# A second attention whose keys are formed beside its values, in one fused kernel of two decoder stages

## The chip, the cores and the metric

One core of a Trainium2 chip runs the whole program. The metric is device time in microseconds, from launch to end, the median of several executions; lower is better. TensorE multiplies, VectorE and ScalarE work on tiles and on TensorE's results, GpSimd (POOL) and SyncE issue transfers. Each engine takes its own instructions in the order written; only semaphores tie one engine to another.

## The reference, cut to what matters

The program computes an even layer (convolution and block attention), an odd layer (the attention of this case), a gated delta rule layer, cross attention and a feed-forward layer, over 256 tokens of width 2048 in float32. The part around the change is the odd layer:

```python
z = _rmsnorm(x, norm_g) @ w_in
cq, ckv, ik, iw, gate = _split_cols(z, [512, 256, 64, 16, 2048])
q = (cq @ w_qb).reshape(b, t, 16, 128)
q_lat = jnp.einsum('bthd,hdc->bthc', q, w_uk)          # 256 latent columns a head
...                                                    # index scores choose 64 keys for each query
s = jnp.einsum('bqhc,bqkc->bqhk', ql_c, kv) * scale
p = jax.nn.softmax(s, axis=-1)
o_lat = jnp.einsum('bqhk,bqkc->bqhc', p, kv)
o = jnp.einsum('bthc,hcd->bthd', o_lat, w_uv).reshape(b, t, DSA_WIDTH)
return (o * jax.nn.silu(gate)) @ w_out
```

There are 16 heads of 128. The scores of a head are q w_uk ckv^T. They can be had by taking q into the latent space (256 wide) and multiplying by ckv, or by taking ckv out to keys of 128 (k = ckv w_uk^T) and multiplying q by those. The choice of keys enters as a bias of -1e30 on what is not chosen; the kernel finds it with 16 rounds of top-8 (8 for each half of the queries).

## The kernel before, in words

**Projections.** Every large weight is split in two float32r halves, a high part (ScalarE's `split`, L1355) and a remainder (VectorE's `split`, L2090), and each product takes three matmuls. A *unit* (L717) is 128 output columns; its result is drained by ScalarE (`drain`, L1371) and summed by VectorE (`post`, L2124). There are two accumulator banks, so a unit waits until the sum of the unit two before it is made (`emptied`, L439). Projections that are added to x are *wide units* (`wide_unit`, L776) of 24 matmuls of 512 columns. Units are handed on through four weight slots: ScalarE splits unit n when unit n-4 has been multiplied.

**The odd layer's order.** `o_small` (cq, ckv, ik, iw), `o_gate0`, `o_iq`, `o_gate1` with the index scores beside it (`index_beside`), then `o_q` (16 units of q, 128 columns each, so one head a unit), the attention loop, and `o_out` (16 wide units). VectorE's `top_k` rounds (L2531) stand between its splits and sums of `o_q`.

**Values beside q.** TensorE forms the values of a later head (`values`, L986: ckv times w_uv, four plain float32 matmuls of 128 columns, each of which the profile shows as two records) behind every second unit of `o_q`, seven heads ahead (`V_AHEAD`), and in the loop's steps those of head s+7. ScalarE copies them out (`values`, L1751).

**The loop** (TensorE L1008, ScalarE L1776, VectorE L2565), one step per head, each engine in its own written order. TensorE's step s: latent queries of head s (L1019, two matmuls of 256 columns); scores of head s-1 from the copied latent queries (L1030); turn of the probabilities of head s-3 (L1039, three transposes); values by probabilities of head s-4 (L1048 and L1049); values of head s+7 (L993). ScalarE's step: copy of the latent queries (L1781), exponential with its sum (L1632), copy of the turned probabilities (`pt_step`, L1641), copy of values (L1756), and in some steps the high part of a unit of `o_out` or of four gated heads (`gate_round`, L1766). VectorE's step: scaling and bias of the scores (`mask_step`, L2401), row maxima (L2405), division by the sum (`scale_step`, L2412 and L2414), product with the gate (L2573), and in some steps the remainder of a unit of `o_out` (L2098) or of four gated heads (`gate_rest`, L2559). Scores of a head wait until the bias of the head two before has been added; probabilities have three places.

The first wide units of `o_out` stand in the last steps (16, 18 and 19): wide unit j needs the gated heads 4j to 4j+3, split.

**Transfers.** POOL loads w_uk and w_uv by head (`load_uk`, `load_uv`, L592 and L598), from when `o_gate1` has been multiplied, and later the gain of the norm behind this layer (L618). SyncE loads the weights of the projections into two ring places.

## Time and profile before

| what | before |
|---|---|
| median of 3 runs | 2435.91 us (2435.5 to 2436.31) |
| the profiled execution | 2435.91 us |
| its span | 2434.2 us |
| TensorE matmuls busy | 2397.7 us, 99% |
| TensorE weight loads busy | 2071.3 us, 85% |
| VectorE busy | 1611.9 us, 66% |
| ScalarE busy | 1166.3 us, 48% |
| POOL busy | 156.6 us, 6% |
| share of TensorE in the chain that ended last | 95% |

The page reads: one row for each engine with its busy time and share of the span; a strip of 40 equal slices with the busy tenths of each engine and the granted clock of TensorE (9 is 90% or more, and all 40 slices have it); the chain that ended last, followed back from the last instruction. Matmul records overlap, since matmuls are pipelined: a matmul's price in a row of matmuls is the distance from one start to the next, not its own duration. In the trace the units of `o_q` end at 653.5 us, the loop's steps run from 654.57 to 728 us, and the other wide units of `o_out` follow.

### The profile page before, as it was taken

The numbers are of one execution on the slowest core, as the hardware profiler recorded it, in microseconds if no ns is written. First come the engines' busy times: TensorE is split into PE (matmuls) and PEld (weight loads), VectorE is DVE, ScalarE is ACT, GpSimd is POOL, SyncE is SP. The second block draws the span as 40 slices with busy tenths as digits, with TensorE's granted clock in tenths as the row PEclk, the third lists the DMA queues.
The fourth block names the chain that finished last, engine by engine and source line by source line (L and its number), as shares of the span: only waits on it lengthen the run. The fifth ranks groups of instructions, "written<-read, shape, count | busy, mean of one in ns | idle before, by whom it ended". The sixth has DMA issues, their size and how long they took to land.

```text
span 2434.2 us, 35338 instructions
## 1 busy us (share of the span) xinstructions
PE 2397.7 (99%) x14059; PEld 2071.3 (85%) x14059; DVE 1611.9 (66%) x2030; ACT 1166.3 (48%) x1407; POOL 156.6 (6%) x142
## 2 busy tenths in 40 slices
PE   7999999999999999999999999999999999999998
PEld 6888988888888888888988888888888888888887
DVE  6999676555665787597665445455777467755764
ACT  6433674545455654643554344345554334433433
POOL 1000000000200100000000000000122002200220
PEclk9999999999999999999999999999999999999999
DMA  8555446454425556553075555444655565656554
GB/s 249 186 194 190 157 139 231 138 191 146 158 86 205 159 177 188 188 159 121 25 251 176 184 195 173 139 146 165 200 180 202 183 200 175 204 178 204 175 183 143
DMA packets 337333, 422.43 MB, mean 174 GB/s; under 512 B 8478, under 2 KB 263212, under 8 KB 336700
## 3 DMA queue, kind: packets, MB, share of 16 engines
q1 hardware_dynamic: 334204, 410.87, 51.4%
q0 software_dynamic: 2544, 8.52, 1.1%
q8 instruction: 89, 1.46, 0.3%
q10 hardware_dynamic: 464, 1.32, 0.2%
q14 instruction: 32, 0.26, 0.0%
HBM read 418.53 MB, written 2.10 MB: 173 GB/s over the span
## 4 chain that ended last, share of the span: by engine, by line
PE 95%; DVE 2%; ACT 1%; DMA 0%; issue 0%; POOL 0%; SPq 0%; ACTq 0%; DVEq 0%
PE ps L742 36%; PE ps L743 18%; PE ps L796 10%; PE ps L798 10%; PE ps L797 10%; PE ps L745 1%; PE ps L747 1%; PE ps L746 1%; PE ps L1075 1%; PE ps L1067 1%; PE ps L993 1%; PE ps L1288 1%; PE ps L1279 1%; PE ps L1030 1%; DMA ring<-in_even_w_in 0%; PE ps L835 0%
## 5 line engine op out<-in xcount | busy, mean ns | idle before, releaser
L742 PE MATMUL ps<-h_cat,w_hi 128*128 128x512 f32 x3840 | 1348.6, 397 | 8.5 <-DVE h_cat L2245 4.5
L743 PE MATMUL ps<-h_cat,w_lo 128*128 128x256 f32 x3840 | 1068.2, 278 | 0.0
L742 PEld LDWEIGHTS ps<-h_cat,w_hi 128*128 128x128 f32 x3840 | 720.9, 188 | 181.2 <-issue 11.2
L743 PEld LDWEIGHTS ps<-h_cat,w_lo 128*128 128x128 f32 x3840 | 723.0, 188 | 2.2 <-issue 1.9
L2102 DVE TENSOR_TENSOR w_lo<-ring,w_hi 128x2048 fp32r<-128x2048 f32 (+2 forms) x279 | 588.4, 2111 | 173.5 <-ACT w_hi L1369 170.7
L1369 ACT ACTIVATE w_hi<-ring 128x2048 fp32r<-128x2048 f32 (+2 forms) x279 | 492.8, 1767 | 88.0 <-PE ps L798 63.2
L2098 DVE TENSOR_TENSOR w_lo<-ring,w_hi 128x2048 fp32r<-128x2048 f32 (+1 forms) x136 | 302.9, 2233 | 229.9 <-ACT w_hi L1366 227.0
L1366 ACT ACTIVATE w_hi<-ring 128x2048 fp32r<-128x2048 f32 (+1 forms) x136 | 252.2, 1862 | 270.9 <-PE ps L798 246.6
L796 PE MATMUL ps<-w_hi,h_cat 128*128 128x512 f32 x640 | 250.7, 392 | 0.0
L798 PE MATMUL ps<-w_hi,h_cat 128*128 128x512 f32 x640 | 249.5, 390 | 0.0
L797 PE MATMUL ps<-w_lo,h_cat 128*128 128x512 f32 x640 | 249.1, 389 | 0.0
L1387 ACT ACTIVATE stage<-ps 128x256 f32<-128x256 f32 x144 | 55.2, 383 | 400.0 <-PE ps L743 399.8
L798 PEld LDWEIGHTS ps<-w_hi,h_cat 128*128 128x128 f32 x640 | 120.2, 188 | 25.1
L797 PEld LDWEIGHTS ps<-w_lo,h_cat 128*128 128x128 f32 x640 | 120.3, 188 | 24.5
L796 PEld LDWEIGHTS ps<-w_hi,h_cat 128*128 128x128 f32 x640 | 120.2, 188 | 24.6
L652 POOL TENSOR_TENSOR fpr<-fsg,cvu 128x512 f32<-128x512 f32 x22 | 71.6, 3253 | 1023.6 <-DVE cvu L2121 1023.6
L796 PE MATMUL ps<-w_hi,act_cat 128*128 128x512 f32 x352 | 137.1, 389 | 0.0
L798 PE MATMUL ps<-w_hi,act_cat 128*128 128x512 f32 x352 | 137.1, 389 | 0.0
L797 PE MATMUL ps<-w_lo,act_cat 128*128 128x512 f32 x352 | 137.0, 389 | 0.0
L2135 DVE TENSOR_TENSOR stage<-stage,ps 128x256 f32<-128x256 f32 x144 | 60.2, 418 | 81.8 <-ACT stage L1387 81.2
L2376 DVE SCALAR_TENSOR_TENSOR conv<-u,prm,conv 128x256 f32<-128x256 f32 x240 | 98.2, 482 | 0.0
L798 PEld LDWEIGHTS ps<-w_hi,act_cat 128*128 128x128 f32 x352 | 66.1, 188 | 13.8
(419 smaller groups left out, 2250.0 us busy)
## 6 DMA issues: line engine op xcount, KB each, us to landing
ring<-in_w_ffn_up SPq DMA_DIRECT2D x44, 2048.0 KB, 8.0
ring<-in_w_mix_in SPq DMA_DIRECT2D x28, 2048.0 KB, 8.3
ring<-in_even_w_in SPq DMA_DIRECT2D x27, 2048.0 KB, 8.0
ring<-in_w_ffn_down SPq DMA_DIRECT2D x16, 2048.0 KB, 8.2
ring<-in_odd_w_in SPq DMA_DIRECT2D x11, 2048.0 KB, 8.4
ring<-in_even_w_out SPq DMA_DIRECT2D x8, 2048.0 KB, 8.0
ring<-in_odd_w_out SPq DMA_DIRECT2D x8, 2048.0 KB, 7.9
ring<-in_w_mix_out SPq DMA_DIRECT2D x8, 2048.0 KB, 8.2
```

What stands on the lines that cost most here:

```text
L652: pool.tensor_tensor(fpr[:], fsg[:], cvu[:], ALU.mult).then_inc(sem["ffn_prod"], 1)
L742: mm(o[:, 0:2 * T], whi[slot][:, k, :], flat(cat[:, k]), start=first, stop=False)
L743: ins = mm(o[:, T:2 * T], wlo[slot][:, k, :], cat[:, k, 0, :], start=False, stop=end)
L796: mm(o[:], rows_of[:, 0, toks], hi, start=first, stop=False)
L797: mm(o[:], rows_of[:, 0, toks], lo, start=False, stop=False)
L798: ins = mm(o[:], rows_of[:, 1, toks], hi, start=False, stop=end)
L1366: af(flat(whi[slot])[:, 0:size], flat(ring[c % RING])[:, u0:u0 + size], ACT.Copy).then_inc(sem["hi_ready"], 1)
L1369: af(whi[slot][:, 0:g.kt, 0:m], chunk(c % RING, g)[:, :, u0:u0 + m], ACT.Copy).then_inc(sem["hi_ready"], 1)
L2098: tt(flat(wlo[slot])[:, 0:size], flat(ring[c % RING])[:, u0:u0 + size], flat(whi[slot])[:, 0:size].bitcast(F32), ALU.subtract).then_inc(se ...
L2102: tt(wlo[slot][:, 0:g.kt, 0:m], chunk(c % RING, g)[:, :, u0:u0 + m], whi[slot][:, 0:g.kt, 0:m].bitcast(F32), ALU.subtract).then_inc(sem["l ...
L2135: tt(z, z, bank(g, n)[:, 0:T], ALU.add).then_inc(sem["summed"], 1)
L2376: ins = stt(o, win, w, o, ALU.mult, ALU.add)
```

## The change

Keys take the place of latent queries. For each head TensorE turns w_uk (two transposes, `uk_turn`), ScalarE copies it out (`ukt_copy`), and TensorE forms values and keys of that head into one bank (`values_keys`: the four matmuls of the values and two of 256 columns for the keys), which ScalarE copies in one operation 512 wide (`vk_copy`). Six heads (`V_AHEAD`) are formed behind every second unit of `o_q`, the rest in the loop's steps, six heads ahead. Scores are then one matmul for each half of the queries, 128 and 256 columns, from q itself. The loop's steps on TensorE become: scores of head s; values and keys of head s+6; turn of w_uk of head s+7; turn of the probabilities of head s-2; values by probabilities of head s-3. On ScalarE: copy of turned probabilities, exponential, copy of values and keys, copy of the turned w_uk, then splits. On VectorE: bias and maxima of head s, scaling of head s-1, product with the gate of head s-3, then splits. The loop has 19 steps in place of 20, the first wide unit moves from step 16 to step 11, the next two stand in steps 16 and 18, and its banks are others. The index heads are added in five steps in place of six, three rounds of top-k move to the last step of `o_gate1`, later rounds are spread otherwise over `o_q`, and the bias is made in step 14 of `o_q`. POOL loads w_uk and w_uv of a head one behind the other, four heads deep.

```diff
--- before.py
+++ after.py
@@ -50,7 +50,8 @@
 A_ODD, A_X = HEADS, HEADS + DSA_HEADS
 FFN_PARTS = [(0, 16), (16, 16), (32, 12)]
 WIDE = 4 * P
-V_AHEAD = 7
+V_AHEAD = 6
+INDEX_AT = ((), (), (0, 1, 2), (3, 4, 5), (6, 7, 8), (9, 10, 11), (12, 13, 14, 15), ())
 NORMS = ("even_norm", "odd_norm", "mix_norm", "x_norm", "mem_norm", "ffn_norm")
...
@@ -307,11 +308,11 @@
     isum = place("isum", [P, P + T], off=SCR + 4 * KB)
     iwork = place("iwork", [P, P + T], off=SCR + 6 * KB)
     top8 = place("top8", [P, TT, 8], off=SCR + 8 * KB)
...
+    UKV, VKS = 4, 12
+    ukv = place("ukv", [P, UKV, 2, KV_LORA], off=H_OFF + 8 * KB)
+    vk_first = place("vk_first", [P, 8, 2, T], off=H_OFF + 16 * KB)
+    vk_more = place("vk_more", [P, VKS - 8, 2, T], off=H_OFF)
+    ukt = place("ukt", [P, 2, KV_LORA], off=AR + 34 * KB)
...
     def gate_group(q):
-        return (gate_cat, 4 * (q // 2)) if q % 2 == 0 else (h_cat, (6, 0)[q // 2])
+        return (gate_cat, 4 * (q // 2)) if q % 2 == 0 else (h_cat, (4, 0)[q // 2])
+    def vk_tile(h):
+        i = h % VKS
+        return vk_first[:, i] if i < 8 else vk_more[:, i - 8]
     def gate_tile(k):
...
+        def load_head(h):
+            if h >= UKV:
+                pool.wait_ge(sem["vk_ready"], h - UKV + 1)
+            pool.dma_start(ukv[:, h % UKV, 0, :], a["odd_w_uk"][0, h]).then_inc(ukv_loaded[h % UKV], 16)
+            pool.dma_start(ukv[:, h % UKV, 1, :].rearrange("p (c d) -> p c d", d=P),
+                           a["odd_w_uv"][0, h].rearrange("(c p) d -> p c d", p=P)).then_inc(ukv_loaded[h % UKV], 16)
         pool.wait_ge(sem["ik_normed"], 1)
         pool.dma_start(ik[IDX_DIM:2 * IDX_DIM, :], ik[IK]).then_inc(sem["ik_copied"], 16)
         pool.wait_ge(sem["acc_ready"], S["o_gate1"].n0 + 8)
...
+        for h in range(DSA_HEADS):
+            load_head(h)
...
     def pair(g, c):
+        if g.name == "o_out" and c == 0:
+            return ps[6:8]
...
-    O_BANKS = (ps[7], ps[1])
-    QL_BOTH = 11
-
...
-        def values(h):
-
-            pe.wait_ge(uv_loaded[h % UVS], 16 * (h // UVS + 1))
+        def uk_turn(h):
+            pe.wait_ge(ukv_loaded[h % UKV], 32 * (h // UKV + 1))
+            if h >= 1:
+                pe.wait_ge(sem["ukt_ready"], h)
+            for ct in range(CKT):
+                cols = slice(ct * P, (ct + 1) * P)
+                ins = nc.tensor.transpose(ps[5][:, cols], ukv[:, h % UKV, 0, cols], ident[:])
+            ins.then_inc(sem["uk_turned"], 1)
+        def values_keys(h):
+            pe.wait_ge(sem["ukt_ready"], h + 1)
             if h >= 2:
-                pe.wait_ge(sem["vd_drained"], h - 1)
+                pe.wait_ge(sem["vk_drained"], h - 1)
+            o = ps[6 + h % 2]
             for kt in range(TT):
+                keys = slice(kt * P, (kt + 1) * P)
                 for ct in range(CKT):
-                    ins = mm(vd_bank(h)[:, kt * P:(kt + 1) * P], ckv[:, ct, kt * P:(kt + 1) * P], uv[:, h % UVS, ct, :],
-                             start=(ct == 0), stop=(ct == CKT - 1))
-            ins.then_inc(sem["vd_ready"], 1)
+                    mm(o[:, keys], ckv[:, ct, keys], ukv[:, h % UKV, 1, ct * P:(ct + 1) * P],
+                       start=(ct == 0), stop=(ct == CKT - 1))
+            for ct in range(CKT):
+                ins = mm(o[:, T:2 * T], ukt[:, h % 2, ct * P:(ct + 1) * P], ckv[:, ct, :],
+                         start=(ct == 0), stop=(ct == CKT - 1))
+            ins.then_inc(sem["vk_ready"], 1)
         def values_beside(j):
-            if j == 2:
+            if j == 3:
                 pe.wait_ge(sem["ckv_normed"], 1)
                 pe.wait_ge(sem["idx_added"], IDX_HEADS)
-            if j >= 2 and j % 2 == 0:
-                values(j // 2 - 1)
+                uk_turn(0)
+            if j >= 4 and j % 2 == 0:
+                values_keys(j // 2 - 2)
+                uk_turn(j // 2 - 1)
         seg("o_q", H_GROUPS["cq_again"], rhs=h_cat, also=values_beside)
-        pe.wait_ge(*emptied(S["o_q"], 16))
-        pe.wait_ge(sem["vd_drained"], V_AHEAD)
-        for s in range(DSA_HEADS + 4):
+        def dsa_scores(h):
+            a_ = A_ODD + h
+            pe.wait_ge(*emptied(S["o_q"], h + 1))
+            pe.wait_ge(sem["vk_drained"], h + 1)
+            pe.wait_ge(sem["masked"], a_ - 1)
+            for qt in range(TT):
+                ins = mm(ps[2 + a_ % 2][:, span(qt)], qo[:, h, qt * P:(qt + 1) * P], vk_tile(h)[:, 1, 0:(qt + 1) * P],
+                         start=True, stop=True)
+            ins.then_inc(sem["scores_ready"], 1)
+        def dsa_turn(h):
+            a_ = A_ODD + h
+            pe.wait_ge(sem["p_ready"], a_ + 1)
+            pe.wait_ge(sem["pt_ready"], a_)
+            for kt in range(TT):
+                for qt in range(kt, TT):
+                    ins = nc.tensor.transpose(ps[4][:, (kt + qt) * P:(kt + qt + 1) * P],
+                                              p_half(a_, qt)[:, kt * P:(kt + 1) * P], ident[:])
+            ins.then_inc(sem["pt_turned"], 1)
+        def dsa_values(h):
+            a_ = A_ODD + h
+            pe.wait_ge(sem["pt_ready"], a_ + 1)
+            if h == 0:
+                pe.wait_ge(*emptied(S["o_q"], 16))
+            pe.wait_ge(sem["o_drained"], a_ - 1)
+            o, v = O_BANKS[h % 2], vk_tile(h)[:, 0]
+            mm(o[:, 0:T], v[:, 0:P], pe_pt[:, a_ % 2, 0, :], start=True, stop=False)
+            mm(o[:, P:T], v[:, P:T], pe_pt[:, a_ % 2, 1, 0:P], start=False, stop=True).then_inc(sem["o_ready"], 1)
+        for s in range(DSA_HEADS + 3):
             if s < DSA_HEADS:
...
+                dsa_scores(s)
             if s + V_AHEAD < DSA_HEADS:
...
+                values_keys(s + V_AHEAD)
+            if s + V_AHEAD + 1 < DSA_HEADS:
+                uk_turn(s + V_AHEAD + 1)
+            if 2 <= s < DSA_HEADS + 2:
+                dsa_turn(s - 2)
+            if s >= 3:
+                dsa_values(s - 3)
+            if s in (11, 16, 18):
+                pe.wait_ge(sem["vk_drained"], DSA_HEADS)
+                wide_unit(S["o_out"], {11: 0, 16: 1, 18: 2}[s], None, H_GROUPS["gate"], None, tile=gate_tile)
+        pe.wait_ge(sem["masked"], A_ODD + DSA_HEADS)
         wide_seg("o_out", tiles_ready=H_GROUPS["gate"], first=3, tile=gate_tile, rows_apart=True)
...
@@ -1748,47 +1748,59 @@
         drain_to(S["o_q"].n0)
         functions_to("o_gate1", 6)
...
+        def vk_copy(h):
+            act.wait_ge(sem["vk_ready"], h + 1)
+            if h >= VKS:
+                act.wait_ge(sem["o_ready"], A_ODD + h - VKS + 1)
+            af(flat(vk_tile(h)), ps[6 + h % 2][:], ACT.Copy).then_inc(sem["vk_drained"], 1)
+        def ukt_copy(h):
+            act.wait_ge(sem["uk_turned"], h + 1)
+            if h >= 2:
+                act.wait_ge(sem["vk_ready"], h - 1)
+            af(ukt[:, h % 2, :], ps[5][:, 0:KV_LORA], ACT.Copy).then_inc(sem["ukt_ready"], 1)
         def values_beside(i, b):
...
+            j = 4 * i + b
+            if j == 6:
+                ukt_copy(0)
+            if j >= 7 and j % 2:
+                vk_copy((j - 7) // 2)
+                ukt_copy((j - 7) // 2 + 1)
+        seg("o_q", values_beside, tail="o_gate1", unrolled=True)
+        drain_to(S["o_out"].n0 - 2)
+        vk_copy(V_AHEAD - 1)
+        ukt_copy(V_AHEAD)
         drain_to(S["o_out"].n0)
         def gate_round(q):
             act.wait_ge(sem["o_drained"], A_ODD + 4 * q + 4)
             if q == 1:
-                act.wait_ge(sem["vd_ready"], DSA_HEADS)
-            else:
-                act.wait_ge(sem["ql_ready"] if q < 3 else sem["scores_ready"], (8, 0, 16, A_ODD + DSA_HEADS)[q])
+                act.wait_ge(sem["vk_ready"], DSA_HEADS)
+            if q % 2 == 0:
+                act.wait_ge(sem["scores_ready"], A_ODD + 4 * q + 8)
             cat, first = gate_group(q)
             af(cat[:, first:first + 4, 0], gate[:, 4 * q:4 * q + 4], ACT.Copy).then_inc(sem["hhi_ready"], 1)
-        for s in range(DSA_HEADS + 3):
+        for s in range(DSA_HEADS + 2):
+            if s >= 2:
+                pt_step(A_ODD + s - 2, pe_pt, ps[4], sem["o_ready"], A_ODD + s - 2)
             if s < DSA_HEADS:
...
+                exp_step(A_ODD + s)
             if s + V_AHEAD < DSA_HEADS:
...
+                vk_copy(s + V_AHEAD)
+            if s + V_AHEAD + 1 < DSA_HEADS:
+                ukt_copy(s + V_AHEAD + 1)
+            if s in (1, 3, 5, 7):
+                split_to(S["o_out"].n0 + (s + 1) // 2)
+            if s in (8, 12, 16):
+                gate_round((s - 8) // 4)
+            if s == 13:
+                split_to(S["o_out"].n0 + 5)
         gate_round(3)
         def mix_squares(c):
@@ -2520,12 +2532,13 @@
         def index_beside(i, b):
             j = 4 * i + b
-            for h in range(3 * j - 6, min(3 * j - 3, IDX_HEADS)) if j >= 2 else ():
+            for h in INDEX_AT[j]:
                 index_add(h)
...
+            if j == 7:
+                dve.wait_ge(sem["idx_added"], IDX_HEADS)
+                ch.link(tt(iwork[:], isum[:], causal[:], ALU.add))
+                top_k(3)
         rounds = [0]
         def top_k(n1):
@@ -2537,18 +2550,27 @@
                                                 in_values=iwork[:, span(qt)], imm_value=TAKEN))
             rounds[0] = max(rounds[0], n1)
-        dve.wait_ge(sem["idx_added"], IDX_HEADS)
-        ch.link(tt(iwork[:], isum[:], causal[:], ALU.add))
+        seg("o_gate0", key_beside, unrolled=True)
+        seg("o_iq")
+        seg("o_gate1", index_beside, unrolled=True, sums_first=True)
         split_to(S["o_q"].n0 + 2)
         post_to(S["o_q"].n0 - 2)
-        top_k(3)
+        top_k(5)
         post_to(S["o_q"].n0 - 1)
         split_to(S["o_q"].n0 + 3)
         dve.wait_ge(sem["hhi_ready"], H_GROUPS["cq_again"] + 1)
         tt(h_lo[:, 0:QT], cq[:], h_hi[:, 0:QT].bitcast(F32), ALU.subtract).then_inc(sem["h_ready"], 1)
-        top_k(6)
         post_to(S["o_q"].n0)
-        seg("o_q", lambda i, b: top_k(min(4 * i + b + 4, 2 * DSA_TOPK // 8)) if 4 * i + b >= 3 else None, unrolled=True)
+        def choose(i, b):
+            j = 4 * i + b
+            if 3 <= j < 14:
+                top_k(min(j + 3, 2 * DSA_TOPK // 8))
+            if j == 14:
+                ch.link(nc.vector.tensor_scalar(iwork[:], iwork[:], 0.5 * TAKEN, NEG, ALU.is_gt, ALU.mult))
+                tt(dbias[:], iwork[:], causal[:], ALU.add).then_inc(sem["top_ready"], 1)
+        seg("o_q", choose, unrolled=True)
         post_to(S["o_out"].n0)
         def gate_rest(q):
@@ -2558,23 +2580,23 @@
             hi_, lo_ = cat[:, first:first + 4, 0], cat[:, first:first + 4, 1]
             tt(lo_, gate[:, 4 * q:4 * q + 4], hi_.bitcast(F32), ALU.subtract).then_inc(sem["h_ready"], 1)
-        ch.link(nc.vector.tensor_scalar(iwork[:], iwork[:], 0.5 * TAKEN, NEG, ALU.is_gt, ALU.mult))
-        tt(dbias[:], iwork[:], causal[:], ALU.add).then_inc(sem["top_ready"], 1)
         dve.wait_ge(sem["top_ready"], 1)
         dve.wait_ge(sem["gated"], S["o_gate1"].g0 + 8)
-        for s in range(DSA_HEADS + 4):
+        for s in range(DSA_HEADS + 3):
+            if s < DSA_HEADS:
+                mask_step(A_ODD + s, dbias, DSA_SCALE)
             if 1 <= s <= DSA_HEADS:
...
+                scale_step(A_ODD + s - 1)
+            if s >= 3:
+                h = s - 3
                 dve.wait_ge(sem["o_ready"], A_ODD + h + 1)
                 tt(gate[:, h, :], gate[:, h, :], O_BANKS[h % 2][:, 0:T], ALU.mult).then_inc(sem["o_drained"], 1)
...
+            if s in (2, 4, 6, 8):
+                split_to(S["o_out"].n0 + s // 2)
+            if s in (9, 13, 17):
+                gate_rest((s - 9) // 4)
+            if s == 14:
+                split_to(S["o_out"].n0 + 5)
         gate_rest(3)
         dve.wait_ge(sem["gain1_loaded"], 16)
```

## Rows read from the trace of the kernel before

**Rows 1.** Busy time in the loop's second half: PE, PEld, DVE, ACT, POOL, clock, DMA.

```profile
689.50:714.00 24.50, 22.75 (x131) 18.60 (x129) 23.02 (x54) 20.43 (x47) 1.07 (x2) 1.00 0.30 97
```

**Rows 2.** TensorE in order of time, one loop step: start, us, what.

```profile
677.34 1.06 PE L993 MATMUL ps<-uv,ckv 128*128 128x128 f32 x8
678.23 1.03 PE L1019 MATMUL ps<-qo,uk 128*128 128x256 f32 x4
679.10 1.47 PE L1030 MATMUL ps<-ckv,qlat 128*128 128x128 f32 x8
680.41 0.49 PE L1039 MATMUL ps<-ident,pe_p 128*128 128x128 f32 x3
680.74 0.60 PE L1048 MATMUL ps<-pe_pt,vd 128*128 128x256 f32 x2
...
681.39 1.06 PE L993 MATMUL ps<-uv,ckv 128*128 128x128 f32 x8
```

**Rows 3.** TensorE: first wide unit, the turn behind it, third wide unit.

```profile
714.19 0.50 PE L796 MATMUL ps<-w_hi,gate_cat 128*128 128x512 f32 x1
...
719.76 0.49 PE L1039 MATMUL ps<-ident,p_third 128*128 128x128 f32 x3
...
728.00 0.47 PE L796 MATMUL ps<-w_hi,gate_cat 128*128 128x512 f32 x1
```

**Rows 4.** TensorE: the waits in and behind the units of q.

```profile
624.69 0.47 PE L742 MATMUL ps<-h_cat,w_hi 128*128 128x512 f32 x1 [1.24 <-DVE gate L2135]
...
651.99 0.47 PE L742 MATMUL ps<-h_cat,w_hi 128*128 128x512 f32 x1 [1.30 <-DVE qo L2135]
...
654.57 1.13 PE L1019 MATMUL ps<-qo,uk 128*128 128x256 f32 x4 [0.93 <-DVE qo L2135]
```

**Rows 5.** ScalarE's copies and exponentials, and TensorE's turn behind one copy.

```profile
661.23 0.36 ACT L1756 ACTIVATE vd<-ps 128x256 f32<-128x256 f32 x1
...
697.41 0.40 ACT L1632 ACTIVATE pe_p<-pe_p,small 128x128 f32<-128x128 f32 x1 [1.14 <-DVE small L2405]
...
698.30 0.47 ACT L1641 ACTIVATE pe_pt<-ps 128x384 f32<-128x384 f32 x1
698.67 1.90 ACT L1366 ACTIVATE w_hi<-ring 128x2048 fp32r<-128x2048 f32 x1
700.48 0.58 ACT L1781 ACTIVATE qlat<-ps 128x512 f32<-128x512 f32 x1
700.95 0.39 ACT L1632 ACTIVATE p_third<-p_third,small 128x128 f32<-128x128 f32 x1
...
698.92 0.52 PE L1039 MATMUL ps<-ident,pe_p 128*128 128x128 f32 x3 [0.53 <-ACT pe_pt L1641]
```

**Rows 6.** VectorE in order of time, the sums beside the units of q.

```profile
626.77 0.42 DVE L2135 TENSOR_TENSOR qo<-qo,ps 128x256 f32<-128x256 f32 x1
...
628.69 0.41 DVE L2135 TENSOR_TENSOR qo<-qo,ps 128x256 f32<-128x256 f32 x1
```

**Rows 7.** ScalarE: the copy that waits for the turn at 719.76.

```profile
720.29 0.49 ACT L1641 ACTIVATE pe_pt<-ps 128x384 f32<-128x384 f32 x1 [4.11 <-PE ps L1039]
```

**Rows 8.** VectorE's masks, split and gate remainder, and ScalarE's exponential between.

```profile
703.72 0.55 DVE L2401 SCALAR_TENSOR_TENSOR pe_p<-ps,dbias 128x384 f32<-128x384 f32 x1
...
705.88 0.56 DVE L2401 SCALAR_TENSOR_TENSOR pe_p<-ps,dbias 128x384 f32<-128x384 f32 x1
...
708.14 2.29 DVE L2098 TENSOR_TENSOR w_lo<-ring,w_hi 128x2048 fp32r<-128x2048 f32 x1
...
712.45 1.22 DVE L2559 TENSOR_TENSOR h_cat<-gate,h_cat 128x1024 fp32r<-128x1024 f32 x1
...
704.95 0.40 ACT L1632 ACTIVATE pe_p<-pe_p,small 128x128 f32<-128x128 f32 x1 [2.16 <-DVE small L2405]
```

**Rows 9.** TensorE's longest idle, and the stretch around its end (clock third last).

```profile
13.19 3.65 PE L835 MATMUL ps<-ident,xs 128*128 128x128 f32 x16 [9.00 <-ACT xs L1537]
...
10.00:14.00 4.00, 0.81 (x4) 0.84 (x5) 1.05 (x3) 3.33 (x8) 0.61 (x1) 1.00 1.20 290
```

More of the change, by code:

```diff
@@ L309, in build @@
     top8 = place("top8", [P, TT, 8], off=SCR + 8 * KB)
-    qlat = place("qlat", [P, 2, CKT, T], off=H_OFF)
-    UKS, UVS, VDS = 4, 8, 12
-    uk = place("uk", [P, UKS, KV_LORA], off=H_OFF + 8 * KB)
-    uv = place("uv", [P, UVS, CKT, P], off=H_OFF + 12 * KB)
-    vd = place("vd", [P, VDS, TT, P], off=H_OFF + 20 * KB)
+    UKV, VKS = 4, 12
[3 more added lines that the diff above has]
+    ukt = place("ukt", [P, 2, KV_LORA], off=AR + 34 * KB)
     qkv = place("qkv", [P, 3 * GH, T], off=AR)
@@ L404, in build @@
     sem = {n: nc.alloc_semaphore(n) for n in names}
-    uk_loaded = [nc.alloc_semaphore(f"uk_loaded{i}") for i in range(UKS)]
-    uv_loaded = [nc.alloc_semaphore(f"uv_loaded{i}") for i in range(UVS)]
+    ukv_loaded = [nc.alloc_semaphore(f"ukv_loaded{i}") for i in range(UKV)]
     loaded = [nc.alloc_semaphore(f"ring_loaded{i}") for i in range(RING)]
@@ L700, in build @@
     PRM_BANK = 4
-    O_BANKS = (ps[7], ps[1])
-    QL_BOTH = 11
-    def vd_bank(h):
-        return ((ps[6], ps[7]) if h < V_AHEAD else (ps[0], ps[5]))[h % 2]
-    def ql_bank(h):
-        return ps[0] if h >= QL_BOTH and h % 2 else ps[6]
+    O_BANKS = (ps[0], ps[1])
     @block.tensor
@@ L2522, in index_beside @@
             j = 4 * i + b
[L2523 removed]
+            for h in INDEX_AT[j]:
                 index_add(h)
[L2526 to L2528 removed]
+            if j == 7:
+                dve.wait_ge(sem["idx_added"], IDX_HEADS)
+                ch.link(tt(iwork[:], isum[:], causal[:], ALU.add))
+                top_k(3)
         rounds = [0]
```

101 lines of the change are left out of this document (1 added, 100 removed).

## The prediction, made before the changed kernel was run

> **What bounds the kernel now.** I read the shares of the page first, then the stretches around the second attention, TensorE's order of work there, and last the waits. TensorE is busy 99% of the span, as the table above has it, so an edit saves only what it takes from TensorE's columns or from its few waits, and every new wait costs in full. The attention loop has two halves. In the first, TensorE has all it needs; in the second (689.5 to 714.0 us) VectorE is busy 23.0 of 24.5 us and TensorE 22.8 [rows 1]: VectorE is the other limit there.
>
> TensorE's order in one step of the loop [rows 2] gives the prices, start to start: latent queries (512 columns) 0.87 us; scores over 256 latent rows (768 columns) 1.31; the turn of one head's probabilities (three transposes) 0.33; probabilities by values 0.66; values of a later head 0.89. A wide unit of the output projection takes 5.57 [rows 3].
>
> I count from the second unit of q at 624.69 [rows 4] to the third wide unit at 728.00 [rows 3]: 103.3 us. The work in it is 15 units of q at 1.39 (20.8), 16 heads at 0.87 + 1.31 + 0.33 + 0.66 + 0.89 (65.0) and two wide units (11.1): 96.9. The other 6.4 us are waits. The profile names 1.3 and 0.9 of them before the loop [rows 4], one of 0.53 behind the copy of turned probabilities [rows 5]; the rest are pieces in the loop's second half.
>
> **TensorE's work.** Each head loses the latent queries (0.87) and half the score columns (384 in place of 768, so 0.65 of 1.31). It gains the keys, two matmuls of 256 columns, which are the latent queries' shape: 0.87. It gains two transposes of w_uk, at 0.11 each from [rows 2]: 0.22. Net -0.43 a head, -6.9 for 16.
>
> **The waits that go.** At q's second unit TensorE waits 1.24 us for a sum that stands behind three rounds of top-k on VectorE [rows 4, 6]. The change puts the sum first. But VectorE, with a remainder, a sum and a 256-wide round to do, then needs 1.92 us from sum to sum (626.77 to 628.69 [rows 6]) for each unit of 1.39, and the next two units, without keys beside them yet, wait about 0.5 each. I take 0 for this part; ends -1.2 (nothing waits) and +0.5 (the three rounds put ahead of the sum of gate unit 5 also hold the last gate unit). The 1.3 at the last unit of q goes, since ScalarE drains unit 13 before it waits for values; the 0.9 before the loop goes, since scores of head 0 need only unit 0. All 6.4 us of old waits are taken off here, and the new waits counted anew.
>
> **The new chain.** This decides. Keys and values of head s+6 wait in TensorE's step s for the turned w_uk of that head, which ScalarE copies at the end of its step s-1. ScalarE's step begins with the copy of turned probabilities, and those come from the transposes that TensorE now has *behind* keys and values. ScalarE takes its work in order, so in one loop step, one after another: keys and values 1.76 (0.89 + 0.87), turn of w_uk 0.22, turn of probabilities 0.33; hand-over to ScalarE 0.20 (transposes start at 719.76, take 0.33, the copy starts at 720.29 [rows 3, 7]); copy 0.37, exponentials 0.89, copy of values and keys 0.47 (512 wide, as the latent copy is), copy of turned w_uk 0.36 [rows 5]; hand-over back 0.15 (copy ends 698.77, transposes start 698.92 [rows 5]). The sum is 4.75. TensorE has 3.62 of work in such a step (1.76 + 0.22 + 0.33 + 0.66 + 0.65), so it waits 1.13 at each. Steps 0 and 1 turn no probabilities, and steps 3 to 9 have the wait: 7 x 1.13 = 7.9. Ends: 1.0 and 1.3 a step, 7 to 9.
>
> What lies beside it: the splits, moved to steps 1 to 8. ScalarE's (1.81 [rows 5]) starts when keys start and ends before the turn, 2.31 behind, so it is hidden. VectorE's (2.29 [rows 8]) holds the next mask until 2.3 us behind the next keys' start with its 1.23 up to the exponential [rows 8], and the exponential can start only at 2.9: hidden by 0.6. If TensorE's chain were shorter these two would show. The same 32 loads of w_uk and w_uv go out from POOL in pairs as a slot frees, three steps (over 10 us) ahead of use, and nobody waits for the present ones: nothing. SyncE's loads of the projection start earlier and find a free queue: nothing.
>
> At the loop's start, keys of head 7 wait for exponential 0 (the last sum, the mask, 1.23, 0.89, then both copies): 0.9, and those of head 8 0.3. Ends 0.5 and 2. Together 1.2.
>
> **The second half.** From step 10 a head costs TensorE 1.64 us and VectorE 2.16 [rows 8], so TensorE waits for VectorE's scaling wherever no wide unit covers it. I laid the steps out with the last keys' start (step 9) as zero. TensorE: 1.76, turn 7 (0.33), values 6 (0.66), scores 10 (0.65), turn 8, values 7, scores 11 (1.64): ready for turn 9 at 5.0. VectorE: the product of head 6 ends 0.3 behind its values and takes 0.33, so 3.4; the first gate remainder 1.22, of which some 0.1 overlaps [rows 8], so mask 10 at 4.5; mask and maxima 1.1, reciprocal and scaling of head 9 0.7 (together with the product's 0.33 the 2.16 of a head [rows 8]), so 6.4, and 0.1 to the restart: 1.5 of waiting. Values 8, then the wide unit of step 11 from 7.5 to 13.1; beneath it VectorE finishes all it has scores for. Then scores 12, turn 10, values 9, scores 13: ready for turn 11 at 15.4, but mask 12 starts at 14.1 (scores 12 and some 0.4 of hand-over, an estimate: twice that of the shorter transposes), scaling 11 ends at 16.0: 0.8. Turn 12 costs 0.5 the same way (2.16 against 1.64). Turn 13 waits behind the second gate remainder: 1.5. Turn 14, in step 16, stands *before* wide unit 1; VectorE has product 11, a split (2.29 [rows 8], less the overlap), mask 15 and scaling 14 to do first: 0.34 + 2.21 + 1.1 + 0.7 = 4.4 against values 12 and restart, 3.35. Wide unit 2 waits for the third remainder, which VectorE has behind the product of head 14, which waits for values 14: 1.2. Sum 8.9. Ends 6 (the splits fall into idle time of VectorE) and 11.
>
> **Sum.** -6.9 - 6.4 + 0 + 7.9 + 1.2 + 8.9 = +4.7; laying the same steps end to end by time gives the third wide unit at 733.4 against 728.0, +5.4, as restarts behind a wait add about 0.1 each. I take +5.0. Behind it TensorE is full, and VectorE's wait for the gain table (now 5 us later) falls beside wide units already split. The profiled execution took 2435.91 us, its span being 2434.2; that is also the median of the runs, so 2435.9 + 5.0 = **2440.9 us**. A measurement here can tell 0.2% (4.9 us) from nothing.
>
> **The rivals.**
> *The chain does not bind* (B). If ScalarE's tail behind the turn took under the 1.31 us of values and scores instead of 2.44, the 7.9 would vanish: 5.0 - 7.9, 2433, ends 2428 and 2436. For it: ScalarE is far from full now. Against it: the order is written out, and every term has a row. It decides from a loop step of 4.0 us down, where the sum passes zero. 0.14.
> *Half of it* (C). The waits of both halves share slack: while TensorE stalls VectorE gets ahead, and the second half gives back 2 to 4 us: 2437 to 2439. For it: 8.9 rests on VectorE being exactly as late as I laid out. 0.22.
> *The forecast* (A), 2439 to 2444: 0.52.
> *The clock falls* (D). At the kernel's start TensorE idles 9.0 us, and the granted clock of the stretch around the idle's end is 1.00, the level of 2.4 GHz [rows 9]; so no wait of 3.35 should lower it. If it fell, half of wide unit 1 to all of it would run at 1.2 GHz: +3 to +6, 2444 to 2447. 0.05. The Trainium skill (TensorE: Matmul & The Clock Gate, Why this matters for your kernels) warns that idle gaps between bursts bring the half-rate clock; the trace's one long gap does not bear that out.
> *Longer hand-overs* (E) than this order's rows show, restarts with them: 2444 to 2446. 0.07.
>
> **Numbers.** Range 2435 to 2446: A, C, E, half of D and the upper end of B. Faster by over 0.2% (under 2431) is half of B: 0.07. Slower by over 0.2% (over 2440.8) is D, E and 0.34 of A, which lies right on that bound, but whose likelier errors are waits left out: 0.46. The rest, 0.47, is within.
>
> **What would show it.** In the changed profile: keys' matmuls behind a wait of 1.0 to 1.2 us on the copy of turned w_uk, seven times, with a period near 4.75; latent-query matmuls gone; score matmuls halved; no wait of TensorE at the last unit of q; a wait of over 3 us before turn 14. Wrong if the period in steps 3 to 9 is under 4.2, if TensorE's waits from q's second unit to wide unit 2 sum to under 14, or if a split shows among what TensorE waits for in the first half.

## The result, and the profile after

The changed kernel takes 2442.38 us (median of 11 runs, 2441.72 to 2443.43), the kernel before beside it 2435.79 (11 runs): the ratio is 1.0027, with a 95% interval of 1.0019 to 1.0036. It is slower by 6.6 us; 2440.9 was predicted, with a range of 2435 to 2446. Its profiled execution took 2442.17.

The page of the changed kernel: span, busy time by engine, chain that ended last by engine.

```profile
span 2440.5 us, 35272 instructions
...
PE 2393.7 (98%) x14027; PEld 2064.4 (85%) x14027; DVE 1611.7 (66%) x2030; ACT 1166.6 (48%) x1407; POOL 156.6 (6%) x142
...
PE 95%; DVE 3%; ACT 2%; DMA 0%; issue 0%; POOL 0%; SPq 0%; ACTq 0%; DVEq 0%
```

TensorE has 4.0 us less busy time than before (2397.7 in the table) and a longer span. So most of the difference is waiting, and the waits of TensorE from the last gate unit to behind the loop say for whom (line waited at, releasing engine and line, us in total, times, longest):

```profile
PE ps L990 <- ACT ukt L1763: 7.5, 8, 1.6
PE ps L1027 <- DVE p_third L2426: 3.4, 2, 3.1
PE ps L1027 <- DVE pe_p L2426: 2.7, 3, 1.4
PE ps L781 <- DVE gate_cat L2581: 0.9, 1, 0.9
PE ps L727 <- DVE qo L2147: 0.5, 2, 0.3
PE ps L727 <- DVE gate L2147: 0.5, 1, 0.5
```

Line numbers are the changed kernel's: L990 are values and L993 keys of a later head, L978 the turn of w_uk, L1027 the turn of probabilities, L1039 and L1040 probabilities by values, L1016 scores, L781 to L783 a wide unit. None of the old waits [rows 4, 5] is in the list but the one for a gate sum, which is 0.5 in place of 1.24. The new list sums to 15.5 us.

**The first half.** One loop step of TensorE in order of time, and ScalarE's work between the two starts (start us, duration, engine, line, what, idle before and its releaser):

```profile
679.22 1.16 PE L990 MATMUL ps<-ukv,ckv 128*128 128x128 f32 x8 [0.89 <-ACT ukt L1763]
680.22 1.03 PE L993 MATMUL ps<-ckv,ukt 128*128 128x256 f32 x4
681.08 0.38 PE L978 MATMUL ps<-ident,ukv 128*128 128x128 f32 x2
681.30 0.49 PE L1027 MATMUL ps<-ident,pe_p 128*128 128x128 f32 x3
...
684.00 1.16 PE L990 MATMUL ps<-ukv,ckv 128*128 128x128 f32 x8 [0.89 <-ACT ukt L1763]
```

```profile
681.83 0.49 ACT L1641 ACTIVATE pe_pt<-ps 128x384 f32<-128x384 f32 x1 [2.66 <-PE ps L1027]
682.21 0.39 ACT L1632 ACTIVATE p_third<-p_third,small 128x128 f32<-128x128 f32 x1
...
683.09 0.58 ACT L1756 ACTIVATE vk_more<-ps 128x512 f32<-128x512 f32 x1
683.57 0.38 ACT L1763 ACTIVATE ukt<-ps 128x256 f32<-128x256 f32 x1
```

The step is the chain laid out in the prediction, start to start: keys and values 1.86, turn of w_uk 0.22, turn of probabilities and hand-over 0.53, copy 0.38, exponentials 0.88, copy of values and keys 0.48, copy of w_uk and hand-over 0.43. From 679.22 to 684.00 that is 4.78. The scores of the next head stand before that wait in TensorE's order, so nothing is left for TensorE to do in it. The first of the seven such waits is longer:

```profile
669.67 1.16 PE L990 MATMUL ps<-ukv,ckv 128*128 128x128 f32 x8 [1.55 <-ACT ukt L1763]
```

It stands in step 3, and the step before it has no values by probabilities (0.66) to fill the round trip.

**The second half.** TensorE at turns 13 and 14, then the start of wide unit 1, and in the second fence VectorE in the same time:

```profile
719.38 0.55 PE L1027 MATMUL ps<-ident,pe_p 128*128 128x128 f32 x3 [1.37 <-DVE pe_p L2426]
...
723.68 0.67 PE L1027 MATMUL ps<-ident,p_third 128*128 128x128 f32 x3 [3.10 <-DVE p_third L2426]
724.13 1.06 PE L1039 MATMUL ps<-pe_pt,vk_first 128*128 128x256 f32 x2
...
725.85 0.63 PE L782 MATMUL ps<-w_lo,h_cat 128*128 128x512 f32 x1
726.27 0.63 PE L783 MATMUL ps<-w_hi,h_cat 128*128 128x512 f32 x1
```

```profile
719.57 2.28 DVE L2110 TENSOR_TENSOR w_lo<-ring,w_hi 128x2048 fp32r<-128x2048 f32 x1
721.77 0.55 DVE L2413 SCALAR_TENSOR_TENSOR pe_p<-ps,dbias 128x384 f32<-128x384 f32 x1
...
723.07 0.55 DVE L2426 TENSOR_SCALAR p_third<-p_third,small 128x128 f32<-128x128 f32 x2
```

Turn 14 waits 3.10 us for the scaling at 723.07, which VectorE has behind a split of 2.28 us and the mask of head 15. That was forecast. What was not is behind it. L1039, 0.60 us long at the other turns, is 1.06 here, and the 512-column matmuls of the wide unit start 0.42 us apart (725.85 to 726.27) and, from 727.72 on, 0.23. The same stretch by windows (start and end, length, busy us and count of PE, PEld, DVE, ACT, POOL, then the granted clock, share and GB/s of DMA):

```profile
720.40:723.60 3.20, 0.18 (x2) 0.00 (x0) 3.13 (x8) 0.65 (x4) 0.00 (x0) 1.00 0.00 0
723.60:725.20 1.60, 1.52 (x6) 1.35 (x7) 1.06 (x5) 1.21 (x4) 0.00 (x0) 0.61 0.04 10
725.20:727.40 2.20, 2.20 (x7) 1.81 (x7) 0.42 (x1) 0.61 (x1) 0.00 (x0) 0.50 0.00 0
727.40:731.80 4.40, 4.40 (x20) 3.56 (x20) 0.00 (x0) 0.00 (x0) 0.00 (x0) 1.00 0.00 0
```

The granted clock is 1.00 up to 723.60, all through the wait, then 0.61 and 0.50, and 1.00 again from 727.40. TensorE ran at 1.2 GHz in place of 2.4 at the start of wide unit 1. The Trainium skill (TensorE: Matmul & The Clock Gate, Why this matters for your kernels) advises against idle gaps between bursts of matmuls, since they bring the half clock back; this trace agrees for the wait of 3.10 us. The loop's other waits, of 1.55 us and less, lowered nothing in it.

Wide unit 2, the row that answers to the third wide unit of [rows 3]:

```profile
734.70 0.47 PE L781 MATMUL ps<-w_hi,gate_cat 128*128 128x512 f32 x1 [0.90 <-DVE gate_cat L2581]
```

It starts at 734.70 in place of 728.00: 6.7 us later, which accounts for the whole difference of the medians (6.6).

### The profile page after: what moved, and what is told of

It is laid out like the page before. It is cut to its first block, busy times and chain, and to the rows that moved or that the text cites. A ratio compares the mean times of both kernels' runs of the same rounds, so it can differ in the third digit from the quotient of the medians.

```text
span 2440.5 us, 35272 instructions
## 1 busy us (share of the span) xinstructions
PE 2393.7 (98%) x14027; PEld 2064.4 (85%) x14027; DVE 1611.7 (66%) x2030; ACT 1166.6 (48%) x1407; POOL 156.6 (6%) x142
## 4 chain that ended last, share of the span: by engine, by line
PE 95%; DVE 3%; ACT 2%; DMA 0%; issue 0%; POOL 0%; SPq 0%; ACTq 0%; DVEq 0%
PE ps L727 36%; PE ps L728 18%; PE ps L781 10%; PE ps L783 10%; PE ps L782 10%; PE ps L730 1%; PE ps L732 1%; PE ps L731 1%; PE ps L1075 1%; PE ps L1067 1%; PE ps L990 1%; PE ps L1288 1%; DVE w_lo L2114 1%; PE ps L1279 1%; PE ps L993 1%; DMA ring<-in_even_w_in 0%
## 5 line engine op out<-in xcount | busy, mean ns | idle before, releaser
L781 PE MATMUL ps<-w_hi,h_cat 128*128 128x512 f32 x640 | 251.0, 392 | 0.0
L783 PE MATMUL ps<-w_hi,h_cat 128*128 128x512 f32 x640 | 249.4, 390 | 0.0
L783 PEld LDWEIGHTS ps<-w_hi,h_cat 128*128 128x128 f32 x640 | 120.4, 188 | 25.2
L781 PEld LDWEIGHTS ps<-w_hi,h_cat 128*128 128x128 f32 x640 | 120.4, 188 | 24.7
L782 PEld LDWEIGHTS ps<-w_lo,h_cat 128*128 128x128 f32 x640 | 120.4, 188 | 24.7
L781 PE MATMUL ps<-w_hi,act_cat 128*128 128x512 f32 x352 | 137.0, 389 | 0.0
L783 PE MATMUL ps<-w_hi,act_cat 128*128 128x512 f32 x352 | 137.0, 389 | 0.0
L781 PEld LDWEIGHTS ps<-w_hi,act_cat 128*128 128x128 f32 x352 | 66.1, 188 | 13.9
```

The costliest lines, as they stand in the source:

```text
L781: mm(o[:], rows_of[:, 0, toks], hi, start=first, stop=False)
L782: mm(o[:], rows_of[:, 0, toks], lo, start=False, stop=False)
L783: ins = mm(o[:], rows_of[:, 1, toks], hi, start=False, stop=end)
```

## The experiments

All times are medians of 5 to 11 runs, with the kernel before run beside them (2435.5 to 2435.8 in each group). Ratios are against that.

**1. Turn and values first.** TensorE's loop step:

```
             if s < DSA_HEADS:
                 dsa_scores(s)
+            if 2 <= s < DSA_HEADS + 2:
+                dsa_turn(s - 2)
+            if s >= 3:
+                dsa_values(s - 3)
             if s + V_AHEAD < DSA_HEADS:
                 values_keys(s + V_AHEAD)
             if s + V_AHEAD + 1 < DSA_HEADS:
                 uk_turn(s + V_AHEAD + 1)
-            if 2 <= s < DSA_HEADS + 2:
-                dsa_turn(s - 2)
-            if s >= 3:
-                dsa_values(s - 3)
```

> The changed kernel with TensorE's loop step reordered: scores, turn of probabilities, probabilities by values, and only then keys and values of a later head and the turn of w_uk. The probabilities are then turned 1.98 us earlier in the step (keys and values 1.76, turn of w_uk 0.22). Theory, the chain over ScalarE's queue sets the first half: the eight waits of 0.89 before values (7.5 us in all with the short one) go, the period of a step falls from 4.77 to TensorE's 3.6 to 3.8, and the time falls by 7 to 8, from 2442.4 to about 2434.5. The clock still falls at the wait before turn 14. Rival, the splits on VectorE and ScalarE would show as soon as the chain is shorter (the step has 3.62 of TensorE work, and a step with a split has 4.4 of VectorE work): the period stays over 4.2 and the time is 2437 to 2440. Second rival, the slack is shared: what the first half saves the second half waits more, 2440 to 2442.

It took 2433.74 us, ratio 0.9991 (0.9982 to 1.0000). Values of two successive heads, then turn 14 and wide unit 2, on TensorE:

```profile
672.30 1.06 PE L990 MATMUL ps<-ukv,ckv 128*128 128x128 f32 x8
...
675.92 1.06 PE L990 MATMUL ps<-ukv,ckv 128*128 128x128 f32 x8
...
714.40 0.90 PE L1027 MATMUL ps<-ident,p_third 128*128 128x128 f32 x3 [3.10 <-DVE p_third L2426]
...
725.13 0.47 PE L781 MATMUL ps<-w_hi,gate_cat 128*128 128x512 f32 x1 [0.89 <-DVE gate_cat L2581]
```

The step is 3.62 us, TensorE's own work and no more; of the chain's waits one of 0.6 is left, in step 1. The second half is as it was, with the wait of 3.10 and the slow clock. So the order inside TensorE's step was worth 8.6 us by the medians, and neither the splits nor VectorE showed in the first half. By the traces it was worth more: turn 14 starts 9.3 earlier than in the changed kernel and wide unit 2 9.6 earlier, yet the span is only 8.2 shorter. The rest was lost behind the attention, where the granted clock fell a second time in this trace (experiment 7 shows the place).

**2. The turn alone first**, values by probabilities left behind keys and values:

```
             if s < DSA_HEADS:
                 dsa_scores(s)
+            if 2 <= s < DSA_HEADS + 2:
+                dsa_turn(s - 2)
             if s + V_AHEAD < DSA_HEADS:
...
-            if 2 <= s < DSA_HEADS + 2:
-                dsa_turn(s - 2)
             if s >= 3:
```

> The changed kernel with only the turn of probabilities moved ahead of keys and values; probabilities by values stay behind them. Theory, the chain goes as with both moved, but VectorE's product of a head now waits for a matmul at the end of the step, its split stands behind the product, and the next mask behind the split: the mask of odd steps is late, the exponential and the copy of turned w_uk behind it, and about every second step still has a wait of 1.0 to 1.4: 2437.5 to 2439.5. Rival, only the place of the turn counts: the same time as with both moved, 2434.5.

It took 2438.13, ratio 1.0009 (1.0000 to 1.0019). TensorE's waits from the loop to wide unit 2:

```profile
PE ps L1027 <- DVE p_third L2426: 3.7, 3, 3.1
PE ps L1027 <- DVE pe_p L2426: 3.3, 4, 1.4
PE ps L990 <- ACT ukt L1763: 2.2, 4, 0.6
```

L990 waits 2.2 us in four places, and VectorE's scalings are late seven times in place of five. The rival falls. A single product that comes later in the step moves the split behind it, and the split the mask: in this trace VectorE waits 1.09 us for such a product, takes it up at 676.12, then has a split of 2.28, so the next mask starts at 678.66 only, and TensorE's turn at 680.63 waits 0.28 for VectorE. So 4.4 us of the 8.6 are lost again.

**3. Copies ahead of the exponentials**, in ScalarE's step alone; TensorE's order stays as changed:

```
             if s >= 2:
                 pt_step(A_ODD + s - 2, pe_pt, ps[4], sem["o_ready"], A_ODD + s - 2)
-            if s < DSA_HEADS:
-                exp_step(A_ODD + s)
             if s + V_AHEAD < DSA_HEADS:
                 vk_copy(s + V_AHEAD)
             if s + V_AHEAD + 1 < DSA_HEADS:
                 ukt_copy(s + V_AHEAD + 1)
+            if s < DSA_HEADS:
+                exp_step(A_ODD + s)
```

> The changed kernel with ScalarE's loop step reordered alone: copy of turned probabilities, copy of values and keys, copy of turned w_uk, and only then the exponentials; TensorE's order stays. Theory, the chain loses the exponentials' 0.89: its terms then sum to 3.86 to 3.88 against 3.62 of TensorE work, so the period of steps 3 to 9 falls from 4.77 to about 3.88 and the time by 7 x 0.89 = 6.2, to 2436.2. Rival, the exponentials are late for VectorE or a split is next in line: period 4.2 to 4.6, 2438 to 2441.

It took 2437.43, ratio 1.0006 (0.9997 to 1.0015). The same four rows of TensorE:

```profile
672.75 1.16 PE L990 MATMUL ps<-ukv,ckv 128*128 128x128 f32 x8
...
676.67 1.16 PE L990 MATMUL ps<-ukv,ckv 128*128 128x128 f32 x8
...
718.30 0.90 PE L1027 MATMUL ps<-ident,p_third 128*128 128x128 f32 x3 [3.10 <-DVE p_third L2426]
...
730.28 0.47 PE L781 MATMUL ps<-w_hi,gate_cat 128*128 128x512 f32 x1 [0.90 <-DVE gate_cat L2581]
```

The step is 3.92, near the 3.88 of the theory. That shows that the wait was the length of ScalarE's queue between turn and copy, since nothing of TensorE's was touched. The time is 1.2 above the theory's. The traces give two parts: turn 14 starts 5.4 us earlier than in the changed kernel, where the theory has 6.2, and from turn 14 to wide unit 2 it is 11.98 us here, 11.02 there (10.73 in experiment 1). The clock was low for longer:

```profile
717.20:722.00 4.80, 3.70 (x12) 3.13 (x13) 2.48 (x10) 2.42 (x6) 0.00 (x0) 0.50 0.01 3
```

**4. Wide unit 1 in step 15**:

```
-            if s in (11, 16, 18):
+            if s in (11, 15, 18):
                 pe.wait_ge(sem["vk_drained"], DSA_HEADS)
-                wide_unit(S["o_out"], {11: 0, 16: 1, 18: 2}[s], ...)
+                wide_unit(S["o_out"], {11: 0, 15: 1, 18: 2}[s], ...)
```

> The changed kernel with wide unit 1 put at the end of step 15 in place of step 16, nothing else. VectorE then has 5.57 us of TensorE work to catch up under before turn 14 is due. Theory, the wait of 3.1 before turn 14 goes and with it the fall of the granted clock behind it, which costs 1.6 (turn 14 to the end of wide unit 1 took 8.14 against 6.57 at full pace): 2442.4 - 4.7 = 2437.7, and wide unit 1 takes 5.57 again. Rival, the slow stretch is no result of the wait: the granted clock falls at the same place or a little later, and the time is 2439.3. Second rival, the wait only moves on to turn 15 or wide unit 2: 2440 to 2442.

It took 2437.83, ratio 1.0008 (0.9999 to 1.0017): 4.6 less than the changed kernel, where 4.7 was expected. TensorE at turn 13, turn 14 and wide unit 2:

```profile
719.77 0.55 PE L1027 MATMUL ps<-ident,pe_p 128*128 128x128 f32 x3 [1.38 <-DVE pe_p L2426]
...
726.31 0.49 PE L1027 MATMUL ps<-ident,p_third 128*128 128x128 f32 x3
...
730.38 0.47 PE L781 MATMUL ps<-w_hi,gate_cat 128*128 128x512 f32 x1 [0.76 <-DVE gate_cat L2581]
```

Turn 14 has no wait now, the clock is 1.00 in the whole stretch, and wide unit 1 with what stands around it runs at full pace. The waits before turn 13 and wide unit 2 stayed.

**5. The wait filled.** Whether the clock falls for want of work, apart from the wait's own cost:

```
+            if s == 16:
+                for _ in range(6):
+                    mm(ps[5][:, 0:T], ident[:], causal[:, 0:T], start=True, stop=True)
             if 2 <= s < DSA_HEADS + 2:
                 dsa_turn(s - 2)
```

> The changed kernel with six added matmuls of 256 columns ahead of turn 14 in step 16, into a bank that nothing reads there (they add work and change no result). The kernel has such a matmul elsewhere, 0.38 us long; the six fill some 2.3 to 2.6 us of the 3.1 us in which TensorE only waits there, and are done before the probabilities come. Theory, the granted clock falls because TensorE has nothing to do for 3 us: it stays at 1.00 now, wide unit 1 takes 5.57 in place of 6.55, turn 14 starts where it did, and the time falls by 1.6 to 2440.8 though work was added. Rival, the clock falls for another reason (the whole second half's light load): no fall of the time, 2442.4, and half clock near 724 to 727 as before.

It took 2440.78 (2440.18 to 2441.45), ratio 1.0022 (1.0013 to 1.0031), in a run where the kernel before took 2435.50: 5.3 above it, against 6.6. TensorE's added matmuls, turn 14 and wide unit 2, and the windows (columns as above):

```profile
720.69 2.75 PE L1051 MATMUL ps<-causal,ident 128*128 128x256 f32 x12
723.95 0.55 PE L1027 MATMUL ps<-ident,p_third 128*128 128x128 f32 x3 [0.51 <-DVE p_third L2429]
...
733.36 0.47 PE L781 MATMUL ps<-w_hi,gate_cat 128*128 128x512 f32 x1 [0.90 <-DVE gate_cat L2584]
```

```profile
720.70:724.00 3.30, 2.79 (x15) 2.13 (x13) 3.23 (x8) 0.75 (x4) 0.00 (x0) 1.00 0.02 5
724.00:727.40 3.40, 3.40 (x18) 2.93 (x19) 1.36 (x5) 1.70 (x4) 0.00 (x0) 1.00 0.00 0
```

Turn 14 still starts when its probabilities come, the granted clock stays at 1.00, and from turn 14 to wide unit 2 it is 9.41 us in place of 11.02. So the slow clock cost the changed kernel 1.6 us in the trace and 1.3 to 1.6 in the medians, and work that is thrown away took it out.

**6. The same matmuls elsewhere** (the control): three of them in step 15, ahead of turn 13.

```
+            if s == 15:
+                for _ in range(3):
+                    mm(ps[5][:, 0:T], ident[:], causal[:, 0:T], start=True, stop=True)
             if 2 <= s < DSA_HEADS + 2:
                 dsa_turn(s - 2)
```

> A control to the run with six added matmuls: three of the same matmuls are added, but ahead of turn 13 in step 15, where TensorE waits 1.37 us for VectorE; the 3.1 us ahead of turn 14 stay empty. Theory, it is the empty 3.1 us that lower the clock: the granted clock is still halved around wide unit 1 for 2.7 to 6.8 us, and the time stays where the changed kernel's is, 2442.0 to 2443.0 (half clock lasted between these bounds in the runs that had it, which is worth 1.3 to 2.6 us). Rival, added matmuls anywhere in the second half keep the clock up: 2440.8 and a clock of 1.00 throughout.

It took 2442.50, ratio 1.0027 (1.0016 to 1.0038), as the changed kernel. Added matmuls, turn 14, wide unit 2, and a window:

```profile
718.10 1.46 PE L1051 MATMUL ps<-causal,ident 128*128 128x256 f32 x6
...
723.95 0.55 PE L1027 MATMUL ps<-ident,p_third 128*128 128x128 f32 x3 [3.10 <-DVE p_third L2429]
...
734.95 0.47 PE L781 MATMUL ps<-w_hi,gate_cat 128*128 128x512 f32 x1 [0.90 <-DVE gate_cat L2584]
```

```profile
725.20:727.40 2.20, 2.20 (x7) 1.72 (x7) 0.42 (x1) 0.77 (x1) 0.00 (x0) 0.50 0.03 7
```

The clock is halved behind an empty 3.10 us although matmuls were added before it. What counts is that this gap is filled, not that work was added.

**7. Both edits** (1 and 4 in one kernel).

> Both earlier edits in one kernel: scores, turn, probabilities by values, then keys and values in TensorE's step, and wide unit 1 at the end of step 15. Measured alone against the changed kernel's 2442.4 they gave -8.6 and -4.6. Theory, the chain of the first half and the wait of the second are separate things and add: 2442.4 - 8.6 - 4.6 = 2429.2, and the clock never falls. Rival, they share slack: VectorE is further behind at step 10 when the first half is shorter, and the sum gives 2431 to 2434.

It took 2428.69, ratio 0.9972 (0.9962 to 0.9983). The two gains add within 0.5 us, so the halves share next to no slack.

The profiled execution took 2430.36, and its trace shows what the stretch of the loop hides. In the layer behind this one TensorE waits 1.42 us for VectorE, and the granted clock falls behind that wait (TensorE, then a window):

```profile
804.97 0.59 PE L727 MATMUL ps<-h_cat,w_hi 128*128 128x512 f32 x1 [1.42 <-DVE h_cat L2257]
...
805.20:808.60 3.40, 3.40 (x14) 2.95 (x14) 3.22 (x10) 2.89 (x7) 0.00 (x0) 0.50 0.05 15
```

The same wait, of 1.41 or 1.42, stands in the trace of every kernel of this case. Only here and in experiment 1 (from 809.00 to 812.60, mean 0.55) does the clock fall behind it; from its end to the fourth group of transposes behind it (L820) it then took 5.78 and 5.91 us, in place of 4.56 in the changed kernel. It also seems to come and go between executions of one kernel: of the eight here, six have a mean granted clock of 0.999 and took 2428.38 to 2428.97, two have 0.998 and took 2429.94 and 2430.36. Experiments 4, 8 and 9 part in the same way, by 0.3 us and more, though where the clock fell in an execution that was not profiled is not on record. So a wait of 3.10 is not needed for the clock to fall; why it falls behind 1.42 us in some executions and not in others was not tried.

**8. Remainders and splits beneath the wide units**, on top of 7 (VectorE's side; ScalarE's halves go the same way):

```
-            if s in (2, 4, 6, 8):
+            if s in (2, 4, 6):
                 split_to(S["o_out"].n0 + s // 2)
-            if s in (9, 13, 17):
-                gate_rest((s - 9) // 4)
-            if s == 14:
-                split_to(S["o_out"].n0 + 5)
+            if s in (8, 11, 15):
+                gate_rest({8: 0, 11: 1, 15: 2}[s])
+            if s in (11, 15):
+                split_to(S["o_out"].n0 + s // 4 + 2)
```

> The kernel with both edits, and the gate's remainders and the splits moved beneath the wide units on VectorE: remainder 0 in step 8, remainder 1 and the fourth split in step 11, remainder 2 and the fifth split in step 15 (were 9, 13, 8, 17, 14), ScalarE's halves of them with them. In the changed kernel the waits behind remainders were 1.12 (turn 9), 1.37 (turn 13) and 0.90 (wide unit 2), those behind the head's 2.16 of VectorE against 1.64 of TensorE 0.32 and 0.24. Theory, VectorE's work is all that is late there and it fits beneath the wide units (2.16 + 1.22 + 2.28 = 5.66 against 5.57): the three waits go, 3.0 to 3.4 less than with both edits, some 2426. Rival, the work beneath a wide unit overruns and the waits move to turns 11 and 15: 2428 to 2429. Second rival, the later split delays the loads of the projection's weights and TensorE waits for them: 2430 or more.

It took 2427.07, ratio 0.9967 (0.9955 to 0.9979), 1.6 less than 7 where 3.0 to 3.4 were expected. TensorE's waits in the loop:

```profile
PE ps L1027 <- DVE pe_p L2426: 1.3, 4, 0.5
PE ps L1027 <- DVE p_third L2426: 1.0, 2, 0.7
```

The wait before turn 13 is 0.24 in place of 1.37, and the one of 0.8 before wide unit 2 is gone, but six waits for a scaling are left, 2.3 us in all (turns 8, 9, 11, 12, 13 and 15). Step 8 has no wide unit, so the first remainder only moved its wait: 0.67 and 0.24 before turns 8 and 9, in place of 0.84 before turn 9. The others are VectorE's 2.10 a head, turn to turn in this trace, against TensorE's 1.64. The theory had left only those before turns 11 and 12 standing (0.56); the result lies half way between it and the first rival (2428 to 2429).

**9. Five heads ahead in place of six**, on top of 8: V_AHEAD is 5, and the units of q form five heads.

> The kernel with both edits and the remainders beneath the wide units, and keys and values formed five heads ahead in place of six: the keys and values of one head move from beside q into step 10 of the loop. TensorE's work is the same. Theory, VectorE (2.16 a head) then catches up in step 10 beneath 3.62 us of TensorE work, and the waits of 0.67 and 0.24 before turns 8 and 9 go, about 1.1 with their restarts: 2427.1 - 1.1 = 2426.0, span near 2424. Rival, the waits move two steps on, or keys that are formed later are late for their scores: 2427 or more.

It took 2426.65, ratio 0.9964 (0.9951 to 0.9978), 0.4 less than 8, which is not clear of the noise (the intervals overlap almost wholly), where 1.1 was expected. In its trace the waits before turns 8 and 9 fell from 0.91 to 0.45 together. This is the lowest median found: 9.1 us under the kernel before, 15.7 under the changed one.

## Why the prediction was right, and where not

The direction, the place and the size held: +6.6 against +5.0. Step by step, against the profiled execution (where a wait is counted from the trace, 0.2 to 0.26 is added to each for the restart, since 0.89 of idle goes with a step of 4.78 for 3.62 of work, and 0.24 with 2.10 for 1.64):

| term | predicted | measured |
|---|---|---|
| loop step, steps 3 to 9 | 4.75 | 4.78 (33.43 over seven) |
| its waits, seven | 7.9 | 8.7 (33.43 less 24.7 of work) |
| loop start | 1.2 | 0.85 + 0.36 = 1.2 |
| turns 9, 11, 12, 13 | 1.5, 0.8, 0.5, 1.5 | 1.35, 0.5, 0.45, 1.6 |
| turn 14 | 3.35 | 3.3 |
| wide unit 2 | 1.2 | 1.1 |
| slow clock | 0 | 1.6 |
| third wide unit starts | 733.4 | 734.70 |

*The work.* The distance from q's second unit (623.87 in the changed kernel) to wide unit 2 is 110.8 us. Work of 96.9 - 6.9 = 90.0, the waits above (18.2), two waits in q with their restarts (0.9) and the clock (1.6) make 110.7, so the -6.9 is right within 0.1. Experiment 1's step of 3.62 is the same sum shown without a wait.

*The chain's waits.* The mechanism and the step's 4.75 were right, but "7 x 1.13 = 7.9" left something out: step 2 turns probabilities and has no values by probabilities yet, so TensorE has 0.66 less to do before the first of the seven waits. The prediction's own chain gives 8.6; 8.7 was measured, with 1.55 of idle at the first (669.67) and 0.89 or 0.90 at the others: the seven steps took 33.43, and the work in them is 7 x 3.62 - 0.66 = 24.7.

*The front.* I took 0 between -1.2 and +0.5. TensorE now waits 0.49 at the last gate unit and no longer 1.24 at the second unit of q, which starts 0.82 earlier; two later units of q wait 0.24 and 0.27, with restarts 0.9 together. Net about 0, as taken. Both old waits of q and loop start are gone, as said.

*Rival B* (the chain does not bind) and *C* (the halves share slack) fall: the period is 4.78, and experiments 1, 4 and 7 add. *E* had no share: the hand-overs are within 0.1 of the rows.

*Rival D, the clock, is what happened*, to about a third of its price, and the step that failed is the one that gave it 0.05: "the granted clock of the stretch around the idle's end is 1.00 ... so no wait of 3.35 should lower it". [Rows 9] could not carry that. They show an idle at the program's start, with no burst of matmuls ahead of it, which is another case than a pause between two bursts. The stretch ended at 14.00, 0.8 us behind the idle, while in the changed kernel the row's clock is still 1.00 for the whole wait and falls only at about 724. And the same rows hold a doubt that I passed over: 16 transposes in 3.65 us, 0.21 each at least, against 0.11 in the loop [rows 2]. Whether they ran at half pace or waited for their rows stays open, but they were no evidence of full pace. What the Trainium skill warns of (TensorE: Matmul & The Clock Gate, Why this matters for your kernels), that idle gaps between bursts bring the half clock, was the better guide for this wait. The size was off too: the half clock lasted 3.4 us in the changed kernel (0.39 missing of 1.60 us at a clock that is halved, so 1.25, and 2.20) and over 6 in experiment 3, and cost 1.3 to 2.6 in place of 3 to 6. With D's 1.6 added to the +5.0 it is +6.6, the measured difference; that this fits to a tenth is luck. Term by term it is the sum's +4.7, 0.8 more at the chain's waits, 0.6 less in the second half (8.3 of 8.9), 0.1 in front and 1.6 by the clock.

*The chances.* "Slower by over 0.2%" had 0.46, "within" 0.47; the result is 0.27%. The forecast sat on the bound, and with the two chances 0.01 apart any larger one for D would have tipped it.

**Where the expected gain went.** The change takes 6.9 us of work and 6.4 of waits from TensorE and 0.8 ahead of q's second unit, and gives back 8.7 in waits behind its own order of the step, 8.3 behind VectorE in the second half, 1.2 at the loop's start, 0.9 in q and 1.6 by the clock. That is 20.7 against 14.1, and wide unit 2 starts 6.7 later. Nothing in that is a price of forming keys: the same change with another order of steps and another place of a wide unit runs at 2428.69, the remainders moved too at 2427.07.
